# Probabilities turned two steps and valued three steps behind their scores, in the attention stages of a two-block forward pass

## The reference, cut to what matters

```python
# dilated attention, group by group; the first group has 16 heads of width 64, dilation 1
s = einsum(q, k) * dh ** -0.5 + bias
p = exp(s - smax); denom = sum(p)
o = einsum((p / denom), v)
# each mixer: three branches on the same 256 tokens
diff  : 8 heads x 2 maps, causal, o = o[map 0] - lam * o[map 1]
mla   : 8 heads, causal
cross : 4 heads on 256 memory rows
out = sum over branches of sigmoid(gate + b_gate) * (branch @ w_branch)
```

## Time and profile before

| what | value |
|---|---|
| median of 3 runs (lowest, highest) | 2388.45 us (2387.96, 2388.94) |
| span of the profiled execution | 2387.5 us |
| median less that span | 0.95 us |
| PE busy | 2351.7 us, 98% of the span |
| DVE, ACT, POOL busy | 1511.0, 1195.5, 283.9 us |
| granted TensorE clock, mean | 0.999 |
| HBM read | 408.31 MB |

### The profile page before, as it was taken

One profiled execution on the slowest core, in us unless ns is written; L12 is line 12 of the kernel. 1 busy time (PEld: TensorE's weight loads), 2 busy tenths in 40 slices (PEclk: granted clock), 3 DMA queues, 4 the chain that ended last, 5 costly groups with the idle time before them and its releaser, 6 DMA issues.

```text
span 2387.5 us, 34279 instructions
## 1 busy us (share of the span) xinstructions
PE 2351.7 (98%) x13900; PEld 2020.1 (85%) x13900; DVE 1511.0 (63%) x2307; ACT 1195.5 (50%) x1794; POOL 283.9 (12%) x247
## 2 busy tenths in 40 slices
PE   9999999999999999999999999999999999999999
PEld 8987778779979977777899887788998887888987
DVE  6555567776555658666665677756665687656654
ACT  4444454454444446444544565555554555554543
POOL 1100010000000000000001121434110122333000
PEclk9999999999999999999999999999999999999999
DMA  7755644466566656544666654445666554445554
GB/s 229 209 194 175 172 125 136 148 187 183 186 194 177 186 185 197 173 134 151 184 186 204 203 177 143 124 126 183 186 199 206 181 170 131 121 144 172 183 189 145
DMA packets 263278, 411.66 MB, mean 172 GB/s; under 512 B 13770, under 2 KB 129370, under 8 KB 263120
## 3 DMA queue, kind: packets, MB, share of 16 engines
q1 hardware_dynamic: 256256, 389.59, 53.2%
q0 software_dynamic: 6432, 19.28, 3.1%
q10 hardware_dynamic: 432, 0.59, 0.1%
HBM read 408.31 MB, written 1.10 MB: 171 GB/s over the span
## 4 chain that ended last, share of the span: by engine, by line
PE 85%; DVE 8%; ACT 4%; issue 1%; POOL 1%; DMA 0%; SPq 0%; ACTq 0%; DVEq 0%
PE banks L1926 16%; PE banks L1928 16%; PE banks L1927 16%; PE banks L1952 9%; PE banks L1961 9%; PE banks L1953 9%; DVE w_lo L2517 2%; ACT w_hi L2205 2%; PE banks L2015 1%; PE banks L2075 1%; PE banks L2028 1%; DVE probs L2712 1%; PE banks L1909 1%; PE banks L1910 1%; PE banks L1915 1%
## 5 line engine op out<-in xcount | busy, mean ns | idle before, releaser
L2517 DVE TENSOR_TENSOR w_lo<-w_raw,w_hi 128x1024 fp32r<-128x1024 f32 x688 | 838.9, 1225 | 618.1 <-ACT w_hi L2205 616.9
L2205 ACT ACTIVATE w_hi<-w_raw 128x1024 fp32r<-128x1024 f32 (+2 forms) x744 | 777.8, 1049 | 534.6 <-PE banks L1928 379.5
L1926 PE MATMUL banks<-w_hi,xt_hi 128*128 128x512 f32 (+2 forms) x1056 | 432.3, 409 | 7.0 <-DVE xt_lo L2545 3.6
L1952 PE MATMUL banks<-xt_hi,w_hi 128*128 128x256 f32 x1728 | 426.5, 283 | 4.7 <-DVE w_lo L2517 3.1
L1953 PE MATMUL banks<-xt_hi,w_lo 128*128 128x256 f32 x1728 | 425.2, 283 | 0.0
L1928 PE MATMUL banks<-w_hi,xt_lo 128*128 128x512 f32 (+2 forms) x1056 | 413.3, 391 | 0.0
L1927 PE MATMUL banks<-w_lo,xt_hi 128*128 128x512 f32 (+2 forms) x1056 | 412.4, 391 | 0.0
L1952 PEld LDWEIGHTS banks<-xt_hi,w_hi 128*128 128x128 f32 x1728 | 326.6, 189 | 6.6 <-DVE w_lo L2517 3.4
L1953 PEld LDWEIGHTS banks<-xt_hi,w_lo 128*128 128x128 f32 x1728 | 326.7, 189 | 0.0
L1926 PEld LDWEIGHTS banks<-w_hi,xt_hi 128*128 128x128 f32 x1056 | 198.9, 188 | 52.3 <-DVE w_lo L2517 9.0
L1961 PE MATMUL banks<-xt_lo,w_hi 128*128 128x256 f32 x1728 | 243.0, 282 | 0.0
(11 more groups left out here) (438 smaller groups left out, 3042.4 us busy)
## 6 DMA issues: line engine op xcount, KB each, us to landing
w_raw<-in_w_mlp SPq DMA_DIRECT2D x128, 512.0 KB, 3.7
w_raw<-in_w_in SPq DMA_DIRECT2D x104, 512.0 KB, 3.7
w_raw<-in_ffn_w_gate SPq DMA_DIRECT2D x88, 512.0 KB, 3.9
w_raw<-in_ffn_w_up SPq DMA_DIRECT2D x88, 512.0 KB, 4.2
w_raw<-in_ffn_w_down SPq DMA_DIRECT2D x88, 512.0 KB, 3.6
w_raw<-in_attn_w_in SPq DMA_DIRECT2D x72, 512.0 KB, 3.8
w_raw<-in_ret_w_in SPq DMA_DIRECT2D x64, 512.0 KB, 3.8
w_raw<-in_ret_w_out SPq DMA_DIRECT2D x16, 512.0 KB, 3.8
```

The lines of the kernel that those rows point to most:

```text
L1926: pe.matmul(bank, xh, wh, start=(c == 0), stop=False)
L1952: pe.matmul(out[f], hi[:, cols], xh, start=(c == 0), stop=False)
L2205: act.activation(k.w_hi[i % SPLIT][:, 0:m], k.raw[i % RAW][:, 0:m], ACT.Copy).then_inc(*ev.mark(k.w_hi_made, ("w_hi", i)))
L2517: dve.tensor_tensor(lo, raw, hi.bitcast(F32), ALU.subtract).then_inc(*ev.mark(k.w_lo_made, ("w_lo", i)))
```

## The change

In `attention` the turn of a head moves from one step behind its scores to two, and its values from two to three. The loop has one step more for each call, and "keep", "divide" and "diff" come one step later with the values.

```diff
-        for i in range(n + 2):
+        for i in range(n + 3):
             if i < n:
                 ...
                 self.step("scores", heads[i], paired)
                 ...
-            if 0 <= i - 1 < n:
-                heads[i - 1].by = self.by_turns()
-                self.step("turn_probs", heads[i - 1])
-            if i >= 2:
-                h = heads[i - 2]
+            if 0 <= i - 2 < n:
+                heads[i - 2].by = self.by_turns()
+                self.step("turn_probs", heads[i - 2])
+            if i >= 3:
+                h = heads[i - 3]
                 self.step("values", h)
                 if h.place == per_bank - 1:
-                    done(h, i - 2 - h.place)
+                    done(h, i - 3 - h.place)
             yield
```

## The result

The changed kernel takes 2398.57 us (median of 4 runs, 2398.16 to 2398.92) where the kernel before took 2388.68 on the same chip. It is slower by 9.9 us, a ratio of 1.0041 with a 95% interval of 1.0027 to 1.0055 (6.4 to 13.1 us). The profiled execution has a span of 2396.9 us, 9.4 more than before.

What follows compares the result with a forecast made beforehand. PE was taken as the bound, busy 2351.7 of 2387.5 us, with 8.7 us of waits aimed at. Sum: -0.1 + 2 x (0 + 0.75 + 0.8) = +3.0, span 2390.5, median 2391.4 us; range 2384 to 2396.5, leaving out 2 in 10.

Steps and rivals of the forecast that it cites:

- Part 2: Mixers' early differential heads: "diff" moves to even steps behind POOL's w_lo, +0.75 us a mixer, bounds -1.15 and +3.0.
- Edits at nothing: Shifted dilated stages, load queues and cross and latent outputs turned three tiles later: all in time, 0 us.
- Part 1: Turn and values one step back: in the mixers, PE's waits for the exponential become waits for ACT's copy, 0 us.
- Part 3: Latent heads' end in each mixer: sigmoids get ahead of the last exponential, two more table loads, +0.8 us a mixer.
- The dilated stage: Its one wait of 0.92 us: the copy goes from DVE to ACT, -0.1 us, bounds -0.9 and +0.9.
- C: Rival: moved "diff" behind POOL's w_lo costs its whole 3.0 us a mixer, plus sigmoids' 0.8; +7.5 us, 2396; chance 0.22.
- B: Rival: the waits go, DVE and ACT have more slack; 2379.8 for all 8.7 us, 2384 for half; chance 0.15.
- the one for the early stretch: Sign at early differential heads: as long or 1 us longer fits the forecast; shrinking 3 us means B, growing 3 us C.
- A: The forecast itself: waits are renamed, small extra costs; 2388 to 2395, chance 0.50.

Runs made afterwards that it cites:

- run 1: Kernel before with the new distance for the 16 differential heads of each mixer alone; 2393.28 us.
- run 9: Changed kernel with "diff" a step later on odd steps, sigmoids behind the last latent exponential and cross heads one tile later, distance kept; 2389.57 us.
- run 6: Changed kernel with each mixer "diff" but the last one step later, on odd steps again; 5.5 us over the kernel before, against 9.9.
- run 4: Changed kernel with the first merge's two sigmoids behind its third weight tile, after the last latent exponential; 2396.32 us.
- run 7: Changed kernel with sigmoids behind the last latent exponential, as in run 4, and cross heads one weight tile later; 1.3 us faster than run 4 by the medians.
- run 2: Kernel before with the new distance for the dilated stage's first group alone; 2389.24 us.
- run 5: Changed kernel with each step's turn of head i - 2 put ahead of the scores of head i; 2390.39 us.
- run 10: Changed kernel with the turn ahead of the scores, "diff" on odd steps and sigmoids behind the last latent exponential; 2387.54 us.
- run 8: Kernel before with the next weight tile made right behind the heads' step, ahead of the mixers' other side work; 2400.5 us.
- run 12: Kernel before's distance, with the turn ahead of the scores and ACT making all copies of the differential heads' turned probabilities; 2394.02 us.

## Why the prediction was wrong, by its steps

The forecast was +3.0 us, 2391.4; the span grew by 9.4 and the median to 2398.57. Two terms of the sum failed. Part 2, the "diff" behind POOL's w_lo, was put at 0.75 us a mixer and measured 2.09. The later cross heads were put at nothing, under "Edits at nothing", and measured 1.23. That is 5.1 us of the 6.4 by which the span was missed. Per mixer unless said:

**Part 1, the mixers (0): right in its sum, with half of the account missing.** The values were to start at about 1489.7 behind the copy; they start at 1489.50, with the whole timeline 0.44 us later by then. The wait was renamed, and what was won ahead of it was given back at it. The L2060 waits went, the copies are 52 by ACT and 20 by DVE as counted:

```profile
L2342 ACT ACTIVATE probs_t<-banks 128x384 f32<-128x384 f32 (+1 forms) x52 | 26.1, 503 | 13.6 <-PE banks L2060 13.6
```

What it does not have is that PE, at any moment that ACT and DVE set, has one turn and one set of values less behind it than before, and does them later, where PE itself is the bound. From the bank wait to the table load the kernel before and run 1 have (PE's busy time and matmuls are the first numbers behind the comma):

```profile
1511.26:1796.26 285.00, 283.88 (x1750) 251.62 (x1751) 175.09 (x271) 154.58 (x263) 73.54 (x46) 1.00 0.55 170
...
1512.29:1798.28 285.99, 284.80 (x1759) 252.49 (x1760) 180.15 (x276) 154.48 (x263) 73.19 (x46) 1.00 0.55 169
```

PE has nine matmuls more, three of a turn and six of values, and is busy for 0.92 us longer, of 0.99 us that this stretch grew. The kernel before has the same size from turn to next tile, 1474.71 - 1473.79:

```profile
1473.79 0.49 PE L2060 MATMUL banks<-ident,probs 128*128 128x128 f32 x3
1474.12 0.83 PE L2075 MATMUL banks<-mx_v,probs_t 128*128 128x128 f32 x6
1474.71 0.48 PE L1926 MATMUL banks<-w_hi,mx_low_t_hi 128*128 128x512 f32 x1
...
1475.73 0.40 PE L1927 MATMUL banks<-w_lo,mx_low_t_hi 128*128 128x512 f32 x1
```

Whether this costs anything hangs on the moment of the bank wait. With the "diff", the sigmoids and the cross heads out of the way (run 9) that moment comes 1.43 us earlier than before, the rest takes 1.62 us longer, and 0.19 is left: the forecast of 0 holds. In the changed kernel the moment is late, nothing is won ahead of it, and the work behind it is paid in full.

**Part 2, "diff" behind w_lo (+0.75, the half of +1.5): the mechanism right, the size wrong.** The bank wait came 1.13 us later in the changed kernel, which looks like the forecast. But with the "diff" back on odd steps (run 6) it came 1.44 us earlier than before, so the move was worth 2.57 us at this point, and 2.09 at the end of the mixer. The sum was made against a bank wait that stays where it is without the move. And the reason given for halving, that each plus supposes a chain without slack, is not borne out: more than the whole +1.5 was paid. L3178 was held in each of the steps 4, 6 and 8, for 1.3 to 2.2 us.

**Part 3, the sigmoids (+0.8): right.** The loads are 16, two more a mixer; PE waits 0.61 us where 0.8 was forecast; taking them away gives 0.72 us by the first mixer of run 4's trace.

**"Edits at nothing" (0): wrong.** The prediction counted the tiles by which the cross heads move and asked only whether their outputs are in time. It did not ask what stands in DVE's and ACT's queues at the tiles to which they move. There are the gate's evacuations: PE waits 1.49 us where it waited 0.33, and moving the heads one tile on gives 1.23 us a mixer (run 7). The bank wait of 0.28 us at 1527.03, behind DVE's mx_gate, is of the same kind.

**The dilated stage (-0.1, once):** +0.54 in the trace, with waits of 0.98 and 0.50 us in place of 0.92; run 2 alone is too small to measure.

The sum can be made in two ways, which count the same microseconds and must not be mixed. By what was taken away: 2.09 (run 6) + 1.23 (run 7) + 0.72 (run 4) + 0.19 (what run 9 keeps) = 4.23 of 4.41. By what was added: 2.14 (run 1, in which the 0.33 us wait is gone and the 0.28 is there) + 1.49 + 0.61 = 4.24 of 4.41. Some 0.2 us a mixer are not found.

**The rivals.** C had the mechanism of Part 2 with its whole price and stayed at 2396; it was the nearest, but it had neither the displaced PE work nor the cross heads. B, that the waits go, could not come true for the reason given against it: the copy behind the exponential in one queue. Run 5, which takes that order away, takes the waits for the copy with it. Of the signs that were to tell, the one for the early stretch (as long as before or 1 us longer, against 3 us or more for C) pointed at A with its 1.13 us, and it was a bad gauge, since it ended where the rest of the loss begins.

## What to carry to other kernels

To give a consumer one more step of distance helps only if what it consumes doesn't stand in a queue behind the very instruction that is late; look at the order inside each engine's queue first, and move the copy ahead of it together with the distance. When a call gets a step longer, everything behind it meets other neighbours: list what stands in each engine's queue at the new tiles, above all long evacuations or sums, and not only who needs the moved result. And work moved past a point that other engines set is not free when the engine that must do it later is the bound: unless that point comes earlier for it, its whole time is added.

## What the runs showed of the chip that was not expected

**Behind some of these idle stretches PE's clock is halved for a while.** In the second mixer the changed kernel has the same wait as in the first (3.00 and 2.98 us). Before the change the longest at the heads was 1.38. The windows of 4 us that begin about there (PEclk is the granted clock):

```profile
core 0: us, PE busy (x) PEld busy (x) DVE busy (x) ACT busy (x) POOL busy (x), PEclk, DMA share, GB/s
1489.00:1493.00 4.00, 3.50 (x18) 2.99 (x19) 2.99 (x9) 3.50 (x11) 1.36 (x1) 1.00 0.30 113
2013.50:2017.50 4.00, 3.96 (x14) 3.45 (x15) 3.45 (x9) 3.50 (x10) 1.83 (x1) 0.60 0.24 94
```

and PE's rows behind the second wait:

```profile
2013.54 1.65 PE L2075 MATMUL banks<-mx_v,probs_t 128*128 128x128 f32 x6 [3.00 <-ACT probs_t L2342]
2014.84 0.77 PE L1926 MATMUL banks<-w_hi,xt_hi 128*128 128x512 f32 x1
2015.41 0.63 PE L1927 MATMUL banks<-w_lo,xt_hi 128*128 128x512 f32 x1
...
2016.69 0.39 PE L1927 MATMUL banks<-w_lo,xt_hi 128*128 128x512 f32 x1
```

A window's mean of 0.60 is PE at 1.2 GHz for most of it and at 2.4 for the rest: matmuls of 0.39 us take 0.63 until 2016.7. The windows behind the same wait in runs 1, 4 and 7 have 0.50 and 0.50, 0.50 and 0.64, 0.64 and 0.66, and behind the 3.07 us of run 5 twice 0.50. In the kernel before, the windows behind its 1.38 us waits have 1.00 in both mixers. But the length of the wait does not decide it. Here are the windows behind the 1.99 us wait of run 10 and behind the 2.84 us wait of run 8 (the clock is the third number from the end):

```profile
1508.77:1512.77 4.00, 4.00 (x14) 3.26 (x15) 0.61 (x4) 3.35 (x8) 4.00 (x4) 0.66 0.00 0
...
1516.42:1520.42 4.00, 4.00 (x23) 3.41 (x24) 1.68 (x2) 3.44 (x8) 2.08 (x3) 1.00 0.32 118
```

Behind the waits of 1.94 and 1.93 us in run 12 the clock is 0.57 and 0.60 as well. Run 9 has two waits of 0.84 and 0.85 us close together in both mixers, and behind them 0.57 in the first and 1.00 in the second. What decides is not explained here.

**It cost nothing here, and says who sets the pace.** In the first mixer the changed kernel stays at the full clock behind this wait and run 1 has 0.50, and yet they take 59.58 and 59.60 us to the bank wait: the next wait for the copy is 2.41 us in one and 0.45 in the other. In the second mixer of the changed kernel the loss can be followed. The six matmuls of the values take 1.30 us until the next starts, and the four after them 1.85, where the kernel before has 0.59 and 1.02 (from 1474.12 to 1474.71 and to 1475.73, in the rows shown with Part 1): 1.5 us lost. But the next wait for ACT's copy is 1.51 us long instead of 2.41. Counted from the offset at which each mixer starts (0.44 and 4.88 us), the values after that wait come 1.09 us later than before in the first mixer and 1.11 in the second. PE was slowed and went on at the same moment, which DVE and ACT had set.
